# Where the loaded halves of 512-column products lie, relative to the streamed ones, modulo 128 words

## The chip, the cores and the metric

The kernel runs on one core of one Trainium2 chip. The metric is the device time of one execution in microseconds (us), smaller is better. Before the change the median of three runs is 1668.29 us (1668.05 to 1669.01).

## What is computed

Two blocks of a network over 256 tokens of width 1024, all in float32. The first block ends with a layer of 16,384 small experts, the second block has two layers that each end in a gated feed-forward part. The change touches the operands of two kinds of products in them, both of which are wide sums of products:

```python
# first block, experts: per token 8 x 16 experts are chosen, each adds coef * its row of expert_up
u = expert_down[eidx]
a = jax.nn.gelu(jnp.einsum('thkd,td->thk', u, xb), approximate=False)
coef = (g * a.astype(jnp.float32)).astype(xb.dtype)
return jnp.einsum('thk,thkd->td', coef, expert_up[eidx])

# second block, at the end of each of its two layers, D_FF = 2816
u, v = jnp.split(hn @ w_up, 2, axis=-1)
...
return (jax.nn.silu(uc) * v) @ w_down
```

## The kernel before

**Split products.** A float32 product runs as three matmuls. Each operand is held as a high part, rounded to the format `fp32r`, and the rest, its low part; the three matmuls are high by high, high by low, low by high, all added in one bank of PSUM. ScalarE (ACT) makes the high parts, VectorE (DVE) the low ones by a subtraction. A matmul of TensorE has two operands in SBUF: the **load**, 128x128 words that are put into the array (rows PEld of the profile), and the **stream**, 128x256 or 128x512 words that pass through it (rows PE). While one matmul streams, the load of the next one runs. In the rows a matmul is written `bank<-stream,load`: `bank<-hi_u,chi` streams `hi_u` and has `chi` loaded.

**First pass and second pass of the experts.** `expert_down` and `expert_up` come in 256 units of 128x1024 words; two units are a pair. In the first pass (units 0 to 127, `down_unit`, lines 940 to 944) a unit is the load and the activations `xh`, `xl` are the stream, 256 columns at a time. In the second pass (units 128 to 255, `up_half`, lines 987 to 989) the coefficients of the pair are the load, and the unit is the stream, 512 columns at a time: for each unit, two blocks of tokens by two halves of the columns by three matmuls, so 12 matmuls, 24 for a pair, 1536 for 64 pairs. The coefficients of pair 0 are `chi0` and `clo0`; those of the others are `chi[:, q % 2]` and `clo[:, q % 2]`, made by ACT in `coef_high` (line 1622) and by DVE in `coef_low` (line 2324). The function `pair_halves(q)` (line 371) hands them to all three. The units' high parts are in `hi_u` (three places), their low parts in `lo_u` and, in the second pass for odd units, in `lo_up` (`low_unit`, line 377).

**Feed-forward parts.** `ffn(layer, res)` first makes the gated activations, whose high and low parts are `gh0`, `gl0` or `gh1`, `gl1` (`gated_of`, lines 408 to 412). Then 11 slots of `w_down` are streamed, 512 columns at a time, with the gated parts loaded: 11 slots by 4 banks by 2 by 3 matmuls, 264 for a layer, 528 for both. All go through the helper `three` (lines 607 to 609).

**Places.** SBUF is laid out by hand with `Area`, counted in words of 4 bytes in each partition. `beside(at, by)` moves the next tensor forward until its place is `at + by` modulo 128. All streamed weights and units (`whi`, `wlo`, `hi_u`, `lo_u`, `lo_up`) are congruent to `HIGH_AT` = 13264, and every slice that a matmul takes of them, or of the loads below, begins a multiple of 128 words into it. What is left is one number for each product, the place of its load minus the place of its stream, modulo 128, called the **offset** here:

| product | stream, load | columns | offset |
|---|---|---|---|
| second pass, lines 987 to 989 | units, `chi` and `clo` | 512 | 0 |
| down product of both layers, lines 607 to 609 | `w_down`, `gh` and `gl` | 512 | 0 |
| first pass, lines 940 to 944 | `xh` and `xl`, units | 256 | 16 |
| `up0`, `up1`, `pq`, `xq` | `nh` and `nl`, weights | 256 | 16 |
| `out`, `xo`, `even_out`, `odd_out` | weights, `xmh` and `xml` | 256 | 16 |
| the last chunks of `in` (`w_v`, `w_o`) | weights, `xh` and `xl` | 256 | 112 |
| `xv` | weights, `memh` and `meml` | 256 | 112 |

What orders the work: TensorE runs its list in program order. In the second pass a unit's high part waits for `unit_used`, which the first matmul of a later unit sets; the coefficients of pair q wait for the unit that last read their place.

Of the kernel before, what the change touches and what calls it, by code (L numbers as in the profile page):

```python
# [29 lines left out]
F32R = mybir.dt.float32r  # L30
# [8 lines left out]
T = 256  # L39
# [158 lines left out]
def program(nc, t):  # L198
    with ExitStack() as ctx:
# [49 lines left out]
        HIGH_AT = keep.at  # L249
# [99 lines left out]
        chi0 = first_pair("chi0", 2, T, dt=F32R)  # L349
        clo0 = first_pair("clo0", 2, T, dt=F32R)  # L350
# [9 lines left out]
        spread_g = units("spread_g", TB, P, P)  # L360
        assert units.at == WORDS
        crossing = Area(CROSSING_AT)
        crossing.beside(HIGH_AT, 0)
        lo_up = crossing("lo_up", UNIT, dt=F32R)
        crossing.beside(HIGH_AT, 0)
        chi = crossing("chi", 2, 2, T, dt=F32R)
        clo = crossing("clo", 2, 2, T, dt=F32R)
        g_final = crossing("g_final", D)
        assert crossing.at <= CROSSING_AT + 2 * KD * T + 128

        def pair_halves(q):
            return (chi0[:, :, :], clo0[:, :, :]) if q == 0 else (chi[:, q % 2, :, :], clo[:, q % 2, :, :])

        def by_block(x):
            return x.rearrange("p c (b t) -> p b c t", b=TB)
# [30 lines left out]

        f5 = Area(ARENA2 + 128)
        gated_of = []
        for layer_, by in ((0, 0), (1, 0)):
            halves = Area(ARENA2)  # L410
            halves.beside(HIGH_AT, by)
            gated_of.append((halves(f"gh{layer_}", 22, T, dt=F32R), halves(f"gl{layer_}", 22, T, dt=F32R)))
# [144 lines left out]
        def _(pe):  # L557
# [424 lines left out]
            def up_half(c, w, half, tb):  # L982
                q, j = c // 2, c % 2
                tok = slice(tb * P, (tb + 1) * P)
                c_hi, c_lo = [x[:, j, tok] for x in pair_halves(q)]
                out, cs = banks[2 * half + tb][:, :], slice(half * 512, (half + 1) * 512)
                first = pe.matmul(out, c_hi, w[0][:, cs], start=(c == 0), stop=False)  # L987
                pe.matmul(out, c_hi, w[1][:, cs], start=False, stop=False)  # L988
                mm = pe.matmul(out, c_lo, w[0][:, cs], start=False, stop=(c == P - 1))  # L989
                if c == P - 1:  # L990
                    cur["b"] = of[2 * half + tb]
                    close(mm)
                return first
# [323 lines left out]
        def _(act):  # L1317
# [299 lines left out]
            def coef_high(q):  # L1617
                act.wait_ge(S("coef_made"), q + 1)
                if q >= 3:

                    act.wait_ge(S("unit_used"), P + 2 * (q - 2) + 2)
                a(A(by_block(pair_halves(q)[0]), spread_g[:, :, 2 * q:2 * q + 2, :], ACT.Copy), S("coef_high"))
# [215 lines left out]
        def _(dve):  # L1838
# [482 lines left out]
            def coef_low(q):  # L2321
                dve.wait_ge(S("coef_high"), q + 1)
                hi, lo = pair_halves(q)
                v(V.tensor_tensor(by_block(lo), spread_g[:, :, 2 * q:2 * q + 2, :], by_block(hi).bitcast(F32), ALU.subtract),
                  S("coef_low"))
# [441 lines left out]
def build(nc, arrays):  # L2767
    t = {}
    for name, a in arrays.items():
        t[name] = nc.dram_tensor(f"in_{name}", a.shape, F32, kind="ExternalInput").ap()  # L2770
    t["aside"] = nc.dram_tensor("aside", (PAIRS, P, 2 * T), F32, kind="Internal").ap()
    t["out"] = nc.dram_tensor("out", (T, D), F32, kind="ExternalOutput").ap()
    program(nc, t)
# [11 lines left out]
```

## Time and profile before

| | |
|---|---|
| median of three runs | 1668.29 us |
| the profiled execution | 1663.66 us |
| its span, first to last instruction | 1661.8 us |
| TensorE busy (PE) | 1643.4 us, 99% |
| VectorE busy (DVE) | 1237.7 us, 74% |
| ScalarE busy (ACT) | 935.5 us, 56% |

All rows are of the profiled execution. It is 4.63 us shorter than the median of the runs. A matmul's own duration in the rows is longer than its share of the time, since a matmul's pipeline overlaps the next; the time that a matmul costs is the distance from its start to the start of the next, called its **step** here. It is read from the starts in the timeline, or from a stretch as its length plus one duration, divided by the matmuls that touch it.

### The profile page before, as it was taken

The page shows a single profiled execution, that of the slowest core. Times are in us where ns is not written, and L with a number is a line of the kernel's source. Part 1 is how long each engine was busy: PE and PEld are TensorE (multiplying, and loading weights), DVE is VectorE, ACT ScalarE, POOL GpSimd, SP SyncE. Part 2 cuts the span into 40 slices and gives each one's busy share as a digit, 9 for nine tenths or more (in the row PEclk, how much of TensorE's full clock was granted, in tenths as well). Part 3 has the DMA queues.
Part 4 walks back from the last instruction along what each step waited for, and adds up shares of the span by engine and source line. Part 5 has one row for each costly group of instructions (what it writes and reads, how often), then busy time and mean ns, then how long its engine had stood idle before and what let it go on. Part 6 is the DMA issues. An engine that isn't in the chain of part 4 may idle for free.

```text
span 1661.8 us, 30280 instructions
## 1 busy us (share of the span) xinstructions
PE 1643.4 (99%) x12006; PEld 1536.2 (92%) x12006; DVE 1237.7 (74%) x1896; ACT 935.5 (56%) x1139; POOL 242.4 (15%) x333
## 2 busy tenths in 40 slices
PE   8999999999999999999999999999999999999999
PEld 8999999999999999988888888999999888899997
DVE  6875467999998666666767767887899565779974
ACT  7786565555555555554554554786655357565542
POOL 0000000004667767301101100000000000100000
PEclk9999999999999999999999999999999999999999
DMA  8444344776555555777777776633555544345553
GB/s 306 153 153 177 106 178 142 236 237 213 188 177 190 186 191 190 270 242 242 240 245 238 240 248 221 234 127 127 194 191 199 190 168 150 127 157 201 202 188 117
DMA packets 73804, 323.40 MB, mean 195 GB/s; under 512 B 8663, under 2 KB 9047, under 8 KB 55744
## 3 DMA queue, kind: packets, MB, share of 16 engines
q1 hardware_dynamic: 58736, 285.18, 50.4%
q0 software_dynamic: 5568, 19.38, 3.8%
q10 hardware_dynamic: 9360, 16.92, 2.7%
q8 instruction: 95, 1.56, 0.4%
q14 instruction: 45, 0.37, 0.1%
HBM read 303.62 MB, written 17.83 MB: 193 GB/s over the span
## 4 chain that ended last, share of the span: by engine, by line
PE 82%; DVE 12%; ACT 4%; issue 1%; DMA 0%; SPq 0%; ACTq 0%; DVEq 0%
PE bank L607 13%; PE bank L609 13%; PE bank L608 13%; PE bank L987 7%; PE bank L988 7%; PE bank L989 7%; PE bank L940 5%; PE bank L944 5%; PE bank L943 5%; DVE lo_u L2301 3%; PE bank L952 2%; DVE wlo L1916 2%; DVE oh L2312 2%; ACT whi L1352 1%; DVE pos L2198 1%
## 5 line engine op out<-in xcount | busy, mean ns | idle before, releaser
L1588 ACT ACTIVATE hi_u<-raw_u 128x1024 fp32r<-128x1024 f32 x256 | 271.9, 1062 | 276.4 <-PE bank L987 160.6
L1916 DVE TENSOR_TENSOR wlo<-raw,whi 128x2048 fp32r<-128x2048 f32 (+1 forms) x141 | 314.7, 2232 | 100.8 <-PE bank L607 77.9
L1352 ACT ACTIVATE whi<-raw 128x2048 fp32r<-128x2048 f32 x137 | 263.2, 1921 | 72.7 <-PE bank L607 69.6
L940 PE MATMUL bank<-xh,hi_u 128*128 128x256 f32 x1024 | 291.6, 285 | 1.3 <-DVE lo_u L2301 0.9
L2301 DVE TENSOR_TENSOR lo_u<-raw_u,hi_u 128x1024 fp32r<-128x1024 f32 x192 | 237.9, 1239 | 67.9 <-PE bank L940 61.6
L943 PE MATMUL bank<-xl,hi_u 128*128 128x256 f32 x1024 | 285.0, 278 | 0.0
L944 PE MATMUL bank<-xh,lo_u 128*128 128x256 f32 x1024 | 284.9, 278 | 0.0
L607 PE MATMUL bank<-nh,whi 128*128 128x256 f32 x904 | 251.7, 278 | 0.7 <-DVE wlo L1916 0.6
L608 PE MATMUL bank<-nl,whi 128*128 128x256 f32 x904 | 250.2, 277 | 0.0
L609 PE MATMUL bank<-nh,wlo 128*128 128x256 f32 x904 | 250.2, 277 | 0.0
L521 POOL TENSOR_SCALAR oh<-kept,sel_T 128x128 f32<-128x128 f32 x256 | 199.5, 795 | 249.2 <-ACT sel_T L1638 165.6
L987 PE MATMUL bank<-hi_u,chi 128*128 128x512 f32 x512 | 199.4, 389 | 0.3 <-DVE lo_up L2301 0.3
L989 PE MATMUL bank<-hi_u,clo 128*128 128x512 f32 x512 | 199.2, 389 | 0.0
L940 PEld LDWEIGHTS bank<-xh,hi_u 128*128 128x128 f32 x1024 | 192.6, 188 | 3.8 <-DVE lo_u L2301 1.7
L943 PEld LDWEIGHTS bank<-xl,hi_u 128*128 128x128 f32 x1024 | 193.5, 189 | 0.0
L944 PEld LDWEIGHTS bank<-xh,lo_u 128*128 128x128 f32 x1024 | 192.7, 188 | 0.0
L607 PEld LDWEIGHTS bank<-nh,whi 128*128 128x128 f32 x904 | 169.8, 188 | 1.7 <-DVE wlo L1916 1.5
L608 PEld LDWEIGHTS bank<-nl,whi 128*128 128x128 f32 x904 | 170.0, 188 | 0.0
L609 PEld LDWEIGHTS bank<-nh,wlo 128*128 128x128 f32 x904 | 169.9, 188 | 0.0
L2301 DVE TENSOR_TENSOR lo_up<-raw_u,hi_u 128x1024 fp32r<-128x1024 f32 x64 | 78.4, 1226 | 94.5 <-PE bank L987 92.9
L607 PE MATMUL bank<-whi,nh 128*128 128x256 f32 x408 | 115.5, 283 | 0.8 <-DVE nl L1897 0.7
L987 PEld LDWEIGHTS bank<-hi_u,chi 128*128 128x128 f32 x512 | 96.1, 188 | 20.6 <-DVE lo_up L2301 0.7
(417 smaller groups left out, 3353.8 us busy)
## 6 DMA issues: line engine op xcount, KB each, us to landing
raw<-in_weights SPq DMA_DIRECT2D x138, 1024.0 KB, 4.8
raw_u<-in_experts SPq DMA_DIRECT2D x256, 512.0 KB, 4.2
aside<-a_out ACTq DMA_DIRECT2D x64, 256.0 KB, 3.7
a_in<-aside POOLq DMA_DIRECT2D x64, 256.0 KB, 3.7
const<-in_const SPq DMA_DIRECT2D x1, 1409.0 KB, 9.0
const<-in_const POOLq DMA_DIRECT2D x1, 1409.0 KB, 7.2
h<-in_x SPq DMA_DIRECT2D x2, 512.0 KB, 5.2
raw<-in_weights SPq DMA_DIRECT2D x2, 512.0 KB, 7.9
```

The source lines that it names most:

```text
L607: freeing(pe.matmul(out, lhs[0], rhs[0], start=first, stop=False, skip_group_check=skip))
L608: pe.matmul(out, lhs[0], rhs[1], start=False, stop=False, skip_group_check=skip)
L609: return pe.matmul(out, lhs[1], rhs[0], start=False, stop=last, skip_group_check=skip)
L940: mm = pe.matmul(out, w[0][:, kp], xh[:, k, :], start=(k == 0), stop=False)
L943: pe.matmul(out, w[0][:, kp], xl[:, k, :], start=False, stop=False)
L944: mm = pe.matmul(out, w[1][:, kp], xh[:, k, :], start=False, stop=(k == KD - 1))
L987: first = pe.matmul(out, c_hi, w[0][:, cs], start=(c == 0), stop=False)
L989: mm = pe.matmul(out, c_lo, w[0][:, cs], start=False, stop=(c == P - 1))
L1352: a(A(whi[:, n % HIGH, :], raw[:, n % RAW, :], ACT.Copy), S("weights_hi"))
L1588: a(A(hi_u[:, u % HIGH_U, :], raw_u[:, u % RAW_U, :], ACT.Copy), S("unit_high"))
L1916: v(V.tensor_tensor(wlo[:, n % LOW, place], raw[:, n % RAW, place], whi[:, n % HIGH, place].bitcast(F32), ALU.subtract), S("weights_split" ...
L2301: v(V.tensor_tensor(low_unit(u), raw_u[:, u % RAW_U, :], hi_u[:, u % HIGH_U, :].bitcast(F32), ALU.subtract), S("unit_split"))
```

## The change

The coefficients of the second pass are no longer two tensors with two places each but `odd_pair` and `even_pair`, each with its high and its low part. `odd_pair` lies at offset 96 and `even_pair` at offset 112; pair 0 keeps `chi0` and `clo0` at offset 0. `lo_up` now lies behind them, at offset 0 to `HIGH_AT` as before. The gated parts lie at offset 64 in layer 0 and at 80 in layer 1. No instruction is added, taken out or reordered, and no wait is changed; only addresses are.

```diff
         crossing = Area(CROSSING_AT)
+        crossing.beside(HIGH_AT, 96)
+        odd_pair = crossing("odd_pair", 2, 2, T, dt=F32R)
+        crossing.beside(HIGH_AT, 112)
+        even_pair = crossing("even_pair", 2, 2, T, dt=F32R)
         crossing.beside(HIGH_AT, 0)
         lo_up = crossing("lo_up", UNIT, dt=F32R)
-        crossing.beside(HIGH_AT, 0)
-        chi = crossing("chi", 2, 2, T, dt=F32R)
-        clo = crossing("clo", 2, 2, T, dt=F32R)
         g_final = crossing("g_final", D)
         assert crossing.at <= CROSSING_AT + 2 * KD * T + 128
 
         def pair_halves(q):
-            return (chi0[:, :, :], clo0[:, :, :]) if q == 0 else (chi[:, q % 2, :, :], clo[:, q % 2, :, :])
+            halves = odd_pair if q % 2 else even_pair
+            return (chi0[:, :, :], clo0[:, :, :]) if q == 0 else (halves[:, 0, :, :], halves[:, 1, :, :])
...
-        for layer_, by in ((0, 0), (1, 0)):
+        for layer_, by in ((0, 64), (1, 80)):
             halves = Area(ARENA2)
             halves.beside(HIGH_AT, by)
```

## Rows read from the trace of the kernel before

**Rows 1.** The page, parts 1 and 2: busy time, TensorE's clock.
```profile
PE 1643.4 (99%) x12006; PEld 1536.2 (92%) x12006; DVE 1237.7 (74%) x1896; ACT 935.5 (56%) x1139; POOL 242.4 (15%) x333
PEclk9999999999999999999999999999999999999999
```

**Rows 2.** The page, part 4: the chain that ended last.
```profile
PE 82%; DVE 12%; ACT 4%; issue 1%; DMA 0%; SPq 0%; ACTq 0%; DVEq 0%
```

**Rows 3.** The page, part 5: costliest groups, two of the second pass.
```profile
L987 PE MATMUL bank<-hi_u,chi 128*128 128x512 f32 x512 | 199.4, 389 | 0.3 <-DVE lo_up L2301 0.3
L989 PE MATMUL bank<-hi_u,clo 128*128 128x512 f32 x512 | 199.2, 389 | 0.0
```

**Rows 4.** Who waited for whom, 691 to 1034 us: in total, times, longest.
```profile
ACT hi_u L1588 <- PE bank L987: 160.6, 122, 1.7
DVE lo_up L2301 <- PE bank L987: 91.4, 62, 1.5
ACT hi_u L1588 <- DMA raw_u<-in_experts: 2.9, 2, 2.7
DVE clo L2324 <- ACT chi L1622: 1.2, 2, 0.7
```

**Rows 5.** Timeline of TensorE in the second pass: start, length, instruction.
```profile
799.82 0.39 PE L987 MATMUL bank<-hi_u,chi 128*128 128x512 f32 x1
...
801.18 0.39 PE L987 MATMUL bank<-hi_u,chi 128*128 128x512 f32 x1
```

**Rows 6.** Stretches of the span, TensorE alone: length, busy time, matmuls; clock; DMA.
```profile
700.00:1030.00 330.00, 330.00 (x1458) 1.00 0.75 243
1309.00:1348.00 39.00, 39.00 (x174) 1.00 0.59 210
1200.00:1280.00 80.00, 80.00 (x708) 1.00 0.55 194
150.00:168.00 18.00, 18.00 (x155) 1.00 0.53 183
59.00:70.00 11.00, 11.00 (x96) 1.00 0.29 97
73.00:78.00 5.00, 5.00 (x46) 1.00 0.63 228
111.00:116.00 5.00, 5.00 (x45) 1.00 0.80 238
177.00:187.00 10.00, 10.00 (x87) 1.00 0.29 107
```

**Rows 7.** Groups by line and form, TensorE alone: the down products of both layers.
```profile
L607 PE MATMUL bank<-whi,gh 128*128 128x512 f32 x176 | 68.8, 391 | 0.0
```

**Rows 8.** One line's instructions, L896: a product of unsplit float32, 256 columns.
```profile
L896 PE MATMUL bank<-xT,vx x32: 379/379/382, 190.1 to 196.8; 128*128 128x256 f32 x32
```

**Rows 9.** Timeline of TensorE, from `up0` into the down product of layer 0.
```profile
1290.43 0.28 PE L607 MATMUL bank<-nh,whi 128*128 128x256 f32 x1
...
1290.77 0.39 PE L607 MATMUL bank<-whi,gh 128*128 128x512 f32 x1
1291.00 0.40 PE L608 MATMUL bank<-wlo,gh 128*128 128x512 f32 x1
1291.23 0.39 PE L609 MATMUL bank<-whi,gl 128*128 128x512 f32 x1
1291.47 0.39 PE L607 MATMUL bank<-whi,gh 128*128 128x512 f32 x1
1291.69 0.39 PE L608 MATMUL bank<-wlo,gh 128*128 128x512 f32 x1
```

**Rows 10.** Timeline of TensorE, the end of a chunk of `out` and the transposes behind it.
```profile
134.03 0.28 PE L609 MATMUL bank<-whi,xml 128*128 128x256 f32 x1
134.15 0.60 PE L594 MATMUL bank<-kept,h 128*128 128x128 f32 x4
```

## The prediction

> **What bounds the kernel now.** I read the busy times first, then the chain of waits, then the stretches of TensorE. TensorE is busy 99% of the span at the full granted clock, which is its level of 2.4 GHz [rows 1], and the chain that ended last is 82% TensorE [rows 2]. So the kernel is a list of matmuls, and what counts is the step from one start to the next. In the second pass no one keeps TensorE waiting: its groups have 0.3 us and 0.0 us of idle time before them [rows 3], while ACT waits 160.6 us and DVE 91.4 us for it between 691 and 1034 us [rows 4]. A change in the steps of that pass therefore moves the end one for one, in both directions, and the same holds for the down products.
>
> The step of a 512-column matmul is steady. From 799.82 to 801.18 us six steps take 1.36 us, 226.7 ns each [rows 5]. Over the whole pass, 700 to 1030 us, it is (330 + 0.389) / 1458 = 226.6 ns; in the down product of layer 0 it is (39 + 0.389) / 174 = 226.4 ns [rows 3, 6]. Both are at offset 0. The 256-column matmuls have **two levels**. In `up0` (offset 16, 1200 to 1280 us) the step is (80 + 0.28) / 708 = 113.4 ns; in `pq` (the same offset, 150 to 168 us) it is (18 + 0.28) / 155 = 117.9 ns. At offset 112 the stretches from 59, 111 and 177 us give 117.5, 117.3 and 118.2 ns, and only the one from 73 us is lower, 5.28 / 46 = 114.8 ns, an upper bound with its edges [rows 6]. I call these the fast and the slow level; between them lie 117.7 - 113.4 = 4.3 ns. The reader should see two things: that the slow level exists at both offsets but is much the more common one at 112 (26 us of 31 in the four stretches), and that 226.6 ns is just two times 113.3 ns.
>
> **The change part by part.** It changes no instruction and no wait, only addresses. The count of steps that it can touch: pairs 1, 3, ... 63 are 32 pairs by 24 = 768 matmuls at offset 96; pairs 2 to 62 are 31 by 24 = 744 at offset 112; 264 each at 64 and 80 in the two down products (176 by 3 = 528 for both [rows 7]). In all 2040. Pair 0, with 24, stays.
>
> *Writing the halves.* ACT and DVE write the same shapes to new addresses. I cost that at nothing: they are covered by the 160.6 and 91.4 us in which these engines wait for TensorE [rows 4]. Without that cover a slower write of a pair's coefficients would count 64 times; DVE waited for ACT's high parts just 1.2 us in all, twice [rows 4].
>
> *`lo_up` moves behind the pairs*, from the place of `xh` to that of `xl`. Both are last read by the first pass's last unit, and the same wait guards it; its offset is unchanged. Nothing.
>
> *The step of 2040 matmuls.* No row shows a 512-column product of this kind at another offset for more than a moment, so it is bounded from both sides.
> From below: if the 226.6 ns hold a stall that another offset removes, what is left is a stream without it. The nearest row is the unsplit float32 product of 256 columns: 31 steps in 196.8 - 190.1 = 6.7 us, 216.1 ns [rows 8]. It passes half as many columns, each slower, so it is a far row, but it is the only full-clock stream of that length with a shorter step. That bounds the gain at 226.6 - 216.1 = 10.5 ns a matmul, 2040 by 10.5 = 21.4 us.
> From above: the load of 128x128 words can slow only the part of the stream beside which it runs. Where a 512-column stretch begins there are rows of just that: the first steps of the down product take 1291.00 - 1290.77 = 0.23, 0.23 and 0.24 us, 0.70 us for three, 233 ns each, and the fourth is back at 0.22 us [rows 9]. That is 6 to 7 ns above the level, and near 113.3 + 117.7 = 231.0 ns, one half of the stream at the slow level and one at the fast. So I price the slow level at 4.3 ns a matmul, one half affected, and at most at 2 by 4.3 = 8.6 ns, both halves: 8.8 us and 17.5 us over 2040.
> The value that I take is **nothing**. The reason is the second thing above: 113.3 ns for 256 columns at offset 16 and 226.6 ns for 512 at offset 0 are the same time per column, although a load runs beside nearly all of the one stream and beside only a part of the other, and at different offsets. A stall between load and stream would not scale with columns. So 226.6 ns reads as a plain rate of the stream, from which no offset can take anything. And in a 512-column stretch the three slow steps cure themselves in under 1 us [rows 9], where a 256-column stretch stays slow for 18 us [rows 6]. The load has about half of the step to spare here; I take it that this slack lets it fall into the fast level at other offsets too.
>
> On this the Trainium skill speaks twice. "TensorE: Matmul & The Clock Gate" (Step-by-step: what each phase is for) says that TensorE has two independent SBUF read ports, so that loading the next weights takes no read bandwidth from the running matmul. By that rule no offset matters and the sum is nothing; the two levels of [rows 6] at one and the same shape speak against its being the whole story. The same page (Back-to-back issue gap) gives N/2.4 + 2.5 ns, an estimate of 215.8 ns for 512 columns; the trace has 226.6. If all of the difference could be had, the sum would be some 22 us.
>
> **Sum.** 0 + 0 + 0: the profiled execution stays at 1663.66 us and the median at 1668.3 us. What may move without a change of step: later 256-column stretches start at another moment and may fall into the other level. The up stages and `even`, `odd` after 1040 us hold about 600 us; if one stretch as long as that of `pq`, 18 us, changes level, that is 155 by 4.3 = 0.7 us; three of them one way are 2 us.
>
> **The rivals.**
> *The slow level takes hold* (slower). Beside the load, the stream runs at the slow level at offsets other than 0. Its place is the first part of each of the 2040 steps, its price 4.3 ns. For it: 26 of 31 us at offset 112 are slow [rows 6], and 744 matmuls go to that offset; and where the last matmul of a chunk has as the next load the transpose's `h`, at offset 48, its step is 134.15 - 134.03 = 0.12 us [rows 10], the slow side of the two levels. Against it: the self-cure above. At all four offsets: 2040 by 4.3 = 8.8 us, 1677.1 us. At 112 alone: 744 by 4.3 = 3.2 us, 1671.5 us. At 112 and 96: 1512 by 4.3 = 6.5 us, 1674.8 us. It decides the sign from 3.3 / 0.0043 = 770 matmuls on. With both halves at all offsets: 1668.3 + 17.5 = 1685.8 us.
> *A stall is removed* (faster). 226.6 ns is not a rate but holds a meeting of load and stream at offset 0, absent at some of 64 to 112. Full price 21.4 us, 1646.9 us; on one of the two kinds of pair, 8 us, 1660.3 us. For it: the float32 row. Against it: the equal time per column.
> *Offsets differ both ways* and cancel: the four values are four different cases, and one number comes out. This falls between the others.
>
> **How the numbers follow.** A measurement of this kernel tells about 0.2%, 3.3 us, from no change. No effect of the offset, or effects on too few matmuls: 0.46, at 1668.3 us, its own range 1666 to 1671. Slow level on 770 matmuls or more: 0.42, most of it 1672 to 1677, a small part to 1686. A removed stall: 0.12, 1647 to 1665. I forecast the first, 1668.3 us. The range leaves out about one in ten on either side: 1664 cuts off the larger gains, 1679 lies above the slow level at all four offsets and below both halves of it.
>
> **What would show it.** Steps of 226.6 ns from 700 to 1030 us (x1458 in that stretch) and in both down products say that I am right. Steps that alternate by pair, every 24 matmuls, say that the offset counts: 231 ns is the slow rival, anything below 226 ns the fast one; the two down products give offsets 64 and 80 by themselves. If the second pass grows and ACT and DVE wait less for TensorE, it is a writer and not the matmul. The prediction is wrong if the load's slack does not let it into the fast level, or if equal time per column was chance.

## The result, and the profile after

The change makes the kernel slower. The median of 16 runs is 1676.32 us (1671.33 to 1679.09), beside 1668.1 us for 16 runs of the kernel before (1661.77 to 1669.43). The ratio is 1.0053, 95% interval 1.0042 to 1.0063, so 8.8 us, between 7.0 and 10.5 us. The profiled execution took 1671.59 us, its span is 1669.8 us, 8.0 us longer than before. Executions of one and the same kernel spread over some 8 us, so where an experiment below has one execution of each kernel (1 to 4, 8 and 9), its time is only a rough sign, and the argument rests on the steps in its trace.

The page's parts 1 and 2, after (the lines that answer to [rows 1]):

```profile
PE 1653.0 (99%) x12006; PEld 1538.0 (92%) x12006; DVE 1237.5 (74%) x1896; ACT 935.5 (56%) x1139; POOL 242.0 (14%) x333
PEclk9999999999999999999999999999999999999999
```

TensorE's busy time grew by 9.6 us with the same 12006 matmuls at the same clock; DVE's and ACT's did not move. Who waited for whom between 691 and 1041 us, after (beside [rows 4]):

```profile
ACT hi_u L1590 <- PE bank L989: 168.7, 123, 1.7
DVE lo_up L2303 <- PE bank L989: 96.2, 63, 1.6
DVE odd_pair L2326 <- ACT odd_pair L1624: 1.2, 2, 0.7
```

ACT and DVE wait longer for TensorE than before (160.6 and 91.4 us, in a pass some 7 us shorter), and DVE waits for ACT's halves 1.2 us as before, so it is not the writers of the halves. The stretches of TensorE, after, in the columns of [rows 6]; the second pass, the down product of layer 0, that of layer 1, and `up0`:

```profile
700.00:1030.00 330.00, 330.00 (x1430) 1.00 0.75 240
1316.00:1354.00 38.00, 38.00 (x169) 1.00 0.59 213
1624.00:1662.00 38.00, 38.00 (x165) 1.00 0.35 126
1200.00:1280.00 80.00, 80.00 (x708) 1.00 0.56 197
```

In the second pass 1430 matmuls stand where there were 1458: 330.39 / 1430 = 231.0 ns a step. Layer 0, at offset 64, has 38.39 / 169 = 227.2 ns; layer 1, at 80, 38.39 / 165 = 232.7 ns. `up0` is as before, 708 matmuls. The timeline of the second pass, after (start, length, instruction), tells the pairs apart:

```profile
810.09 0.39 PE L990 MATMUL bank<-lo_u,odd_pair 128*128 128x512 f32 x1
...
812.89 0.39 PE L990 MATMUL bank<-lo_up,odd_pair 128*128 128x512 f32 x1
...
813.80 0.39 PE L991 MATMUL bank<-hi_u,even_pair 128*128 128x512 f32 x1
...
817.92 0.39 PE L991 MATMUL bank<-hi_u,even_pair 128*128 128x512 f32 x1
```

Twelve steps of an odd pair take 2.80 us, 233.3 ns each; eighteen of an even pair 4.12 us, 228.9 ns each; before, both took 226.7 ns [rows 5]. Taken over all starts of the profile, the means are:

| steps | before | after | count | cost |
|---|---|---|---|---|
| odd pairs, offset 96 | 226.7 ns | 233.0 ns | 768 | 4.8 us |
| even pairs, offset 112 | 226.7 ns | 229.1 ns | 744 | 1.8 us |
| down product of layer 0, offset 64 | 226.9 ns | 226.9 ns | 264 | 0 |
| down product of layer 1, offset 80 | 226.8 ns | 233.3 ns | 264 | 1.7 us |

The sum is 8.3 us, beside the 8.0 us by which the span of the profiled execution grew, and inside the interval of the runs.

These are means. Single steps alternate in a pattern: by their starts to the nanosecond, an odd pair at 96 takes 229 and 237 in turn, an even pair at 112 takes 226, 229 and 232, layer 1 at 80 takes 230 or 231 and 236, where offset 0 has only 226 and 227. The last step of an odd pair takes 232 in place of 237 ns, and that is why 96 shows 233.0 and not 233.3 over all starts.

### The profile page after: what moved, and what is told of

It reads as the page before. It is cut to its first block, busy times and chain, and to the rows that moved or that the text cites. A ratio compares the mean times of both kernels' runs of the same rounds, so it can differ in the third digit from the quotient of the medians.

```text
span 1669.8 us, 30280 instructions
## 1 busy us (share of the span) xinstructions
PE 1653.0 (99%) x12006; PEld 1538.0 (92%) x12006; DVE 1237.5 (74%) x1896; ACT 935.5 (56%) x1139; POOL 242.0 (14%) x333
## 4 chain that ended last, share of the span: by engine, by line
PE 82%; DVE 12%; ACT 4%; issue 1%; DMA 0%; SPq 0%; ACTq 0%; DVEq 0%
PE bank L609 13%; PE bank L610 13%; PE bank L611 13%; PE bank L991 7%; PE bank L990 7%; PE bank L989 7%; PE bank L942 5%; PE bank L945 5%; PE bank L946 5%; DVE lo_u L2303 3%; PE bank L954 2%; DVE wlo L1918 2%; DVE oh L2314 2%; ACT whi L1354 1%; DVE pos L2200 1%
## 5 line engine op out<-in xcount | busy, mean ns | idle before, releaser
L610 PE MATMUL bank<-wlo,nh 128*128 128x256 f32 x408 | 113.2, 277 | 0.0
L611 PE MATMUL bank<-whi,nl 128*128 128x256 f32 x408 | 113.1, 277 | 0.0
L989 PE MATMUL bank<-hi_u,odd_pair 128*128 128x512 f32 x256 | 101.3, 396 | 0.2 <-DVE lo_up L2303 0.2
```

The costliest lines, as they stand in the source:

```text
L610: pe.matmul(out, lhs[0], rhs[1], start=False, stop=False, skip_group_check=skip)
L611: return pe.matmul(out, lhs[1], rhs[0], start=False, stop=last, skip_group_check=skip)
```

## The experiments

The theory after the result: a 512-column step depends on the offset of the load from the stream and on nothing else of their places. The stream's own place is the same modulo 128 in all 512-column products of all runs here; only the load was moved. So for 512 columns no run tells the offset from the place of the load alone. For 256 columns the rows do: with the loads at the place of `HIGH_AT` and the stream 16 words below it (`up0`), and with the stream there and the loads 16 words above (`out`), the same 113.3 ns is reached for long, and with both at that place (experiment 7) the step is 120.0 ns. What else was open: is it the offset or the tensor's place; over which distance does it repeat; which of the two, the load or its own matmul, pays; and is offset 0 good for 256 columns too.

**1. Two values exchanged, and 32 and 48.**

```diff
-        crossing.beside(HIGH_AT, 96)
-        odd_pair = crossing("odd_pair", 2, 2, T, dt=F32R)
-        crossing.beside(HIGH_AT, 112)
+        crossing.beside(HIGH_AT, 48)
         even_pair = crossing("even_pair", 2, 2, T, dt=F32R)
...      # lo_up, as in the change
+        crossing.beside(HIGH_AT, 32)
+        odd_pair = crossing("odd_pair", 2, 2, T, dt=F32R)
...
-        for layer_, by in ((0, 64), (1, 80)):
+        for layer_, by in ((0, 80), (1, 64)):
```

> Second pass: odd pairs at offset 32, even pairs at 48; down product of layer 0 at 80, of layer 1 at 64 (the two values of the change, exchanged). Theory A, the step depends on the offset modulo 64: 32 gives what 96 gave (233.0 ns), 48 what 112 gave (229.1 ns), layer 0 rises to 233.3 ns and layer 1 falls to 226.8 ns. Theory B, it depends on the distance of load and stream either way round modulo 128: 32 gives 233.0 ns like 96, 48 gives 233.3 ns like 80; the layers as in A. Theory C, the places or the layers differ and not the offsets: layer 0 stays at 226.9 ns and layer 1 at 233.3 ns. By A the second pass lasts 356 us, by B 358 us; the whole by A is 8 us above the kernel before.

Measured: 1671.31 us, 7.5 us above the kernel before on the same chip. Stretches of TensorE: the second pass, layer 0, layer 1.

```profile
700.00:1030.00 330.00, 330.00 (x1430) 1.00 0.75 240
1317.00:1355.00 38.00, 38.00 (x165) 1.00 0.57 204
1624.00:1662.00 38.00, 38.00 (x169) 1.00 0.37 135
```

The counts of the two layers are those of the changed kernel, exchanged: 165 matmuls now stand in layer 0 and 169 in layer 1. So it is the place of the load and not the layer or the tensor; theory C falls. Over all starts, odd pairs at 32 have 233.0 ns, as at 96, and even pairs at 48 have 229.1 ns, as at 112. That is theory A, a period of 64 words; by theory B 48 should have given the 233.3 ns of 80.

**2. The other half of the map.** Odd pairs at 64, even pairs at 16, `((0, 32), (1, 48))` for the layers, in the lines of the diff above.

> Second pass: odd pairs at offset 64, even pairs at 16; down product of layer 0 at 32, of layer 1 at 48. Theory A (offset modulo 64): 64 gives 226.7 ns, 16 gives 233.3 ns like 80, layer 0 233.0 ns, layer 1 229.1 ns. Theory B (distance either way, modulo 128): 64 gives 226.7, 16 gives 229.1 like 112, layer 0 233.0, layer 1 233.3 ns. Theory D, that 16 is harmless since 256-column products run at 113.4 ns there: 16 gives 226.7 ns. By A the even pairs cost 744 x 6.6 = 4.9 us, by B 1.8 us, by D nothing.

Measured: 1670.00 us, 6.2 us above the kernel before (one execution each). The timeline of the second pass:

```profile
813.33 0.39 PE L989 MATMUL bank<-hi_u,even_pair 128*128 128x512 f32 x1
...
818.00 0.39 PE L991 MATMUL bank<-hi_u,even_pair 128*128 128x512 f32 x1
818.23 0.39 PE L989 MATMUL bank<-hi_u,odd_pair 128*128 128x512 f32 x1
...
820.29 0.39 PE L989 MATMUL bank<-hi_u,odd_pair 128*128 128x512 f32 x1
...
823.01 0.39 PE L989 MATMUL bank<-hi_u,odd_pair 128*128 128x512 f32 x1
```

Offset 16 costs as much as 80: twenty steps in 4.67 us, 233.5 ns. Theories B and D fall. The odd pairs at 64 do reach the low step, 2.72 us for twelve, 226.7 ns, but only after the first nine steps of the pair, which take 2.06 us, 229 ns each: after the change of offset the pair has lost about 20 ns before it settles. Over all starts 64 has 227.9 ns here, 16 has 233.3 and layer 1 at 48 has 229.1. Layer 0 at 32 has 232.4 ns, 0.6 less than the odd pairs at 32 and 96; its steps run in a longer pattern of seven (228 to 241 ns), and why is not known.

**3. One part of a pair moved.** The edit against the changed kernel; the layers are at `((0, 112), (1, 96))`.

```diff
         crossing.beside(HIGH_AT, 96)
-        odd_pair = crossing("odd_pair", 2, 2, T, dt=F32R)
-        crossing.beside(HIGH_AT, 112)
-        even_pair = crossing("even_pair", 2, 2, T, dt=F32R)
         ...
+        odd_high = crossing("odd_high", 2, T, dt=F32R)
+        even_low = crossing("even_low", 2, T, dt=F32R)
+        crossing.beside(HIGH_AT, 0)
+        odd_low = crossing("odd_low", 2, T, dt=F32R)
+        even_high = crossing("even_high", 2, T, dt=F32R)
```

> Only one part of a pair's coefficients is moved. Odd pairs: high part at offset 96, low part at 0. Even pairs: high part at 0, low part at 96. Down products: layer 0 at 112, layer 1 at 96. If the cost arises where the load of the next matmul runs beside a stream, it lies on the steps whose next load is moved: in odd pairs on L989 and L991 (next load high), not on L990 (next load low), so about (233 + 227 + 233) / 3 = 231 ns on average; in even pairs on L990 alone, (227 + 233 + 227) / 3 = 229 ns. If it arises with a matmul's own load, the odd pairs are slow on L989 and L990 and the even ones on L991. If it is a matter of one pair's parts lying together, it is gone. Layer 0 at 229.1 ns and layer 1 at 233.0 ns, if the pass and the down products obey one rule.

Measured: 1675.17 us, 11.4 us above the kernel before (one execution each). Stretch of the second pass, and an even pair in the timeline (the three lines of a product are L990 to L992 in this kernel):

```profile
700.00:1030.00 330.00, 330.00 (x1421) 1.00 0.74 239
```

```profile
816.22 0.39 PE L990 MATMUL bank<-hi_u,even_high 128*128 128x512 f32 x1
...
820.38 0.39 PE L990 MATMUL bank<-hi_u,even_high 128*128 128x512 f32 x1
```

The second pass has 330.39 / 1421 = 232.5 ns a step, 231.0 in the changed kernel. The two are not alike, since the even pairs of the changed kernel are at 112; with both parts of every pair at 96 it would be 233.0. The 18 steps shown of an even pair take 4.16 us, 231.1 ns each. Over all starts the three lines have 226.7, 232.5 and 235.0 ns in the even pairs (231.4 in the mean) and 233.6, 232.7 and 234.5 in the odd ones (233.6). So an odd pair with one part moved is no shorter than one with both.

Taken apart: in an even pair the step beside which the moved low part is loaded (L991 here) is slow, and the first is not, as expected of a meeting of stream and next load; but L992, beside which an unmoved part is loaded, is slower still. In an odd pair all three are slow. So neither expectation holds. Whether a step pays for the load before it, as its own matmul or as an after-effect like the one at the start of a pair in experiment 2, is left open. The layers at 112 and 96 have 229.2 and 232.4 ns, as the layers at 48 and 32 in experiment 2.

**4. Between the multiples of 16.** Odd pairs at 8, even pairs at 72, layers at 40 and 120.

> Offsets between the multiples of 16. Second pass: odd pairs at 8, even pairs at 72; down product of layer 0 at 40, of layer 1 at 120. If only blocks of 16 words count, 8 behaves like 0 or 16 (226.7 or 233.3 ns) and 72 like 64 or 80 (the same two), 40 like 32 or 48, 120 like 112 or 0. If the step varies smoothly with the offset, 8 and 72 lie near 230 ns, 40 near 231 and 120 near 228 ns. By Theory A 8 and 72 are equal.

Measured: 1676.52 us, 12.8 us above the kernel before (one execution each). Second pass, layer 0, layer 1:

```profile
700.00:1030.00 330.00, 330.00 (x1416) 1.00 0.75 238
1321.00:1359.00 38.00, 38.00 (x165) 1.00 0.58 208
1629.00:1667.00 38.00, 38.00 (x164) 1.00 0.35 126
```

330.39 / 1416 = 233.3 ns, the same for 8 and for 72, which is the period of 64 again; 40 and 120 have 233.3 ns too. So the map is no smooth curve and no matter of blocks of 16: of the places tried, 0 has 226.7 ns, 48 has 229.1, 32 has 232.4 to 233.0, and all others have 233.3.

**5. All wide products at 64.** Both pairs and both layers at 64.

> The change with 64 in place of 96, 112 and 80: both pairs and both down products at offset 64, 256-column products as before. Theory A: steps of 226.7 ns in the whole second pass and both down products, time as the kernel before within 0.1%. If pairs laid out the new way, or lo_up's new place, cost anything by themselves, it is the excess here: up to 8 us.

```profile
700.00:1030.00 330.00, 330.00 (x1458) 1.00 0.75 244
```

Measured: 1664.21 us (median of 12), ratio to the kernel before 1.0002 (0.9992 to 1.0012). The stretch holds the 1458 matmuls of [rows 6]. The new layout of the pairs and `lo_up`'s new place cost nothing that the interval shows (2.0 us at most), and 64 is as good as 0.

**6. The pairs alone.** 96 and 112 for the pairs, both layers back at 0.

> One part of the change alone: pairs at 96 and 112, both down products back at offset 0. From the profile of the changed kernel: 768 x 6.3 ns + 744 x 2.4 ns = 6.6 us longer than the kernel before, and 264 x 6.5 ns = 1.7 us shorter than the change. Second pass of 356 us. If later 256-column stretches matter more than the steps themselves, the difference to before lies outside 5 to 8 us.

Measured: 1670.01 us (median of 6), ratio 1.0033 (1.0020 to 1.0046), so 5.5 us (3.3 to 7.7) where the steps give 6.6. The second pass has 1429 matmuls in the stretch of 330 us, and the layers are at 226.9 and 226.8 ns. The part of the layers is 1.7 us by its steps. What is left of the whole 8.8 us is 3.3 us; the intervals of the two ratios, about 2 us either way each, hold the 1.7 but do not show it.

**7. 256 columns at 0, and at 64.** The kernel before, with `xh`, `xmh`, `memh`, `nh1` and `nh4` to `nh7` and their low parts at one place:

```diff
-        for n_, by in ((4, 16), (5, -16), (6, 16), (7, -16)):
+        for n_, by in ((4, 0), (5, 0), (6, 0), (7, 0)):
-        m1.beside(HIGH_AT, -16)
+        m1.beside(HIGH_AT, 0)
-        p3.beside(HIGH_AT, -16)
+        p3.beside(HIGH_AT, 0)
-        keep.at += 64
+        keep.at += 80
         XH = keep.at
...
-        keep.at += 64
-        mixed = Area(XH + 32)
+        keep.at += 48
+        mixed = Area(XH)
```

The second kernel has them all at 64 by the same lines. What was expected, for 0 and for 64:

> The kernel before, with the 256-column products too at offset 0 (before they were at 16, and at 112 in a few chunks); 512-column ones stay at 0. In the profile of before some 2960 of 8430 steps of 256 columns stand at the slow level, 4.3 ns above the fast one, 12.7 us in all. Theory A carried over (0 modulo 64 is where the load costs the stream nothing, whatever the width): nearly all steps at 113.3 ns, the kernel 8 to 13 us shorter than before, about 1656 us. Rival E (at 256 columns the load fills the step, and the level is set by how a stretch begins, not by the offset): share of slow steps and time as before, 1668 us. Rival F (16 was the better place for 256 columns): more slow steps, up to 23 us longer if all are slow.

> As the kernel with all 256-column products at offset 0, but at 64; 512-column ones stay at 0. By a period of 64 words its time is that of the kernel with 0, within 2 us, and its shares of slow steps are alike. If the period holds only at 512 columns, the two differ.

Measured: 1695.99 us and 1696.13 us (five executions each), ratio 1.0189 for both (1.0174 to 1.0204). I had hoped to gain 8 to 13 us and lost 31.6. Stretches of the kernel with 0, `up0` and `pq`:

```profile
1205.00:1285.00 80.00, 80.00 (x669) 1.00 0.54 193
150.00:168.00 18.00, 18.00 (x152) 1.00 0.50 179
```

80.28 / 669 = 120.0 ns. Of some 8500 steps, 7845 with 0 and 7852 with 64 are 120 ns to the nanosecond: a third level, above both of [rows 6]. Over the starts the 256-column steps are 44.5 us longer in the trace of the kernel with 0 than before, and its span 31.9 us: the other 12.6 us are made up for in the other products and in steps that hold a wait. The period of 64 words holds at 256 columns too, but the map is another: the place that is best for 512 columns is the worst seen here. Theory A carried over and rival E fall. Rival F was right, and its "up to 23 us" too low, as I had priced it with the level of 117.7 ns.

**8. The map of 256 columns.** `by` 24, -8, 40 and 8 for `nh4` to `nh7`, and `xh` at -32, in the lines of the diff above.

> The kernel before with its 256-column products at other offsets, one in each stage; 512-column ones stay at 0. First pass and the first chunks of in at 32, even at 24, up0 at 8, odd at 40, up1 at 56; pq, the memory products and the residual products stay at 16. Known so far at 256 columns: 0 and 64 give 120.0 ns always, 16 gives 113.3 or 117.7 ns by stretch, 112 (48 modulo 64) mostly 117.7 ns. Theory G (a stream loses when it meets the load, and the further the load lies from 0 modulo 64, the less): 32 is the best, 113.3 ns throughout the first pass, which is then some 6 us shorter; 24 and 40 nearly so; 8 and 56 lie between 117 and 120 ns. Theory H (only blocks of 16 words count): 24 behaves like 16 or 32, 8 and 56 like 0 or 16. Theory I (16 alone is good): every other value gives 117 ns or more, and the kernel is 10 to 20 us longer than before.

Measured: 1683.61 us, 15.4 us above the kernel before (one execution each). Stretches: `up0` at 8, `up1` at 56.

```profile
1205.00:1285.00 80.00, 80.00 (x678) 1.00 0.53 185
1500.00:1580.00 80.00, 80.00 (x687) 1.00 0.57 198
```

They give 118.4 and 116.9 ns. Over all starts: the first pass at 32 has 119.5 ns, `even` at 24 has 117.8, `odd` at 40 has 119.9. Theories G and H fall: 32 is near the worst, and 8 and 56 have levels of their own. Theory I holds but for its "117 ns or more", which 56 passes by a hair (116.7 ns), and for offset 112 (48 modulo 64), where the kernel before has one stretch of 46 steps at 113.3 ns (73 to 78 us) that has not come back in any later kernel. Only 16 reaches that level for long. No version that beats the kernel before came out of this.

**9. The second pass cut to 256 columns.** The same tensors, each stream in two parts of 256 columns with a load each; odd pairs at 0 and even ones at 16, then at 32 and 48, the layers at 0.

```diff
-                first = pe.matmul(out, c_hi, w[0][:, cs], start=(c == 0), stop=False)
-                pe.matmul(out, c_hi, w[1][:, cs], start=False, stop=False)
-                mm = pe.matmul(out, c_lo, w[0][:, cs], start=False, stop=(c == P - 1))
+                for part in range(2):
+                    o = out[:, part * T:(part + 1) * T]
+                    cs = slice(half * 512 + part * T, half * 512 + (part + 1) * T)
+                    ...   # the same three matmuls, into o
```

> Width changed, everything else kept: in the second pass each 512-column stream is cut into two of 256 columns, each with its own load, over the same tensors (3072 matmuls in place of 1536). Odd pairs at offset 0, even pairs at 16; down products as before. Theory W (the width decides which offset costs): the odd pairs take 120.0 ns a step, 2 x 120.0 = 240.0 ns in place of 226.7; the even pairs 113.3 to 117.7 ns, 2 x 113.3 = 226.7 ns in place of the 233.3 that 512 columns take there, so the order of 0 and 16 turns round. The pass lasts 350 + 768 x 13.3 ns = 360 us with even pairs at the fast level, 367 us at the slow one. Rival P (it lies in these tensors or this pass): offset 0 is still the shorter one.

> The same cut of the second pass into 256-column streams, odd pairs at offset 32, even pairs at 48. By the map of 256 columns (first pass at 32: 119.5 ns; memory products at 48: 117.8 ns) the odd pairs take 119.5 ns and the even ones 117.8 ns a step. Rival: the map of 256 columns was a matter of its stages, then the steps are others.

Measured: 1687.93 us with 0 and 16, 1678.42 us with 32 and 48, beside 1669.06 us for the kernel before (one execution each). The timeline of the first:

```profile
802.06 0.28 PE L993 MATMUL bank<-hi_u,odd_pair 128*128 128x256 f32 x1
...
807.70 0.28 PE L996 MATMUL bank<-hi_u,odd_pair 128*128 128x256 f32 x1
807.82 0.28 PE L993 MATMUL bank<-hi_u,even_pair 128*128 128x256 f32 x1
```

The pair at 0 takes 5.76 us for 48 steps, 120.0 ns each; over all starts the pairs at 16 have 117.8 ns, those at 32 and 48 have 118.7 and 117.8. So in the very tensors where 0 beats 16 at 512 columns (226.7 against 233.3 ns), 16 beats 0 at 256 (2 by 117.8 against 2 by 120.0 ns). It is the width, with the load that each part has, that turns the order round. The even pairs stayed at the slow of the two levels of offset 16 throughout.

The map, mean step in ns over all starts of a stage, all from the kernels above:

| offset modulo 64 | 0 | 8 | 16 | 24 | 32 | 40 | 48 | 56 |
|---|---|---|---|---|---|---|---|---|
| 512 columns | 226.7 | 233.3 | 233.3 | | 232.4 to 233.0 | 233.3 | 229.1 | 233.3 |
| 256 columns | 120.0 | 118.3 | 113.3 or 117.7 | 117.8 | 118.7 to 119.5 | 119.9 | 117.8, once 113.3 | 116.7 |

## Why the prediction was right or wrong

**What bounds the kernel.** Right. TensorE's list of matmuls is the kernel, and 8.3 us of longer steps made the span 8.0 us longer.

**Which costs were nothing.** Right for the writers of the halves and for `lo_up`: experiment 5 has all of that and the time of before.

**The step.** Here the forecast failed. I took nothing as the value, and the step that failed is the last of that part, "I take it that this slack lets it fall into the fast level at other offsets too". The changed kernel and experiments 1 to 4 show in its place a step that is fixed by where the load lies: 233.3 ns at 80, 233.0 at 96 and 229.1 at 112, and no stretch at these ever settled at 226.7 ns. The slack itself was not read from a row. The rows of the loads, before, in the second pass and in `up0`:

```profile
L987 PEld LDWEIGHTS bank<-hi_u,chi 128*128 128x128 f32 x485 | 91.0, 188 | 18.9
L607 PEld LDWEIGHTS bank<-nh,whi 128*128 128x128 f32 x236 | 44.3, 188 | 0.0
```

A load is recorded with 188 ns beside steps of 226.7 and of 113.3 ns alike. Beside the short step it cannot all be time that the load keeps to itself, so these rows do not say how much of a step is spare, half or less. The self-cure that I read off [rows 9] is real: by their starts to the nanosecond those three steps take 232, 232 and 231, then 227. But it took place at offset 0, and in experiment 2 too a pair settles at the step of its own offset; it tells nothing of another one.

The reason ahead of it, that 113.3 and 226.6 ns are the same time per column at different offsets, was half right. No offset that was tried gave 512 columns less than 226.7 ns, so the faster rival found no support. But I compared 256 columns at 16 with 512 at 0, which are the lowest values found in each map. At one and the same offset the time per column is not equal: at 0 it is 120.0 against 226.7 ns, at 16 it is 113.3 or 117.7 against 233.3. The equality is one of the two lowest values, and I read it as if the offset did not matter.

**The rivals.** The slower one took place. Its number for all four offsets, 1677.1 us, is 0.8 us from the median, but its terms were wrong and met in the sum: it had 4.3 ns for each of 2040 matmuls, and the four offsets cost 0 (at 64), 2.4 (at 112), 6.3 (at 96) and 6.5 ns (at 80). That the number came out is luck. It leaned on the rows of 256 columns at 112; by those rows 112 is worse than 16, and 0 was never seen, while at 512 columns 112 is the mildest of the three that cost, and 0 at 256 columns is the worst. A map of one width says nothing of the other. "At 112 alone" would have been 744 by 2.4 = 1.8 us. The fourth rival, that the four values differ, was right that they are different cases, and wrong that they could cancel: one is zero, three are losses.

**The range**, 1664 to 1679 us, held the median of 1676.3 us only since it reached to that rival; the inner range of the value that I forecast, 1666 to 1671 us, did not.

**What would show it.** Steps that alternate by pair, each 24 matmuls, and two layers with two values: this is what the trace has, and it priced four offsets in one profile.

On the rule that I weighed: the Trainium skill, "TensorE: Matmul & The Clock Gate" (Step-by-step: what each phase is for), has loads and streams on independent read ports, with no bandwidth taken from the running matmul. The runs here differ: addresses alone move a 512-column step between 226.7 and 233.3 ns and a 256-column one between 113.3 and 120.0 ns. The formula of the same page's section "Back-to-back issue gap", an estimate of 215.8 ns for 512 columns, was reached at no offset; the lowest mean is 226.7 ns.

## What to carry to other kernels

Where TensorE is the bound and each matmul has its own load, as in these `fp32r` products (no other format was tried), the distance of the load's address from the stream's, modulo 64 words, is worth up to 3% of a 512-column step (233.3 against 226.7 ns) and up to 6% of a 256-column one (120.0 against 113.3 ns). It has to be measured for each width: in this kernel 0 is the place for 512 columns and 16 for 256. One profile maps several offsets at once, if different stages or alternating buffers get different ones; and a level read off one width or one offset should not be carried to another without a run.

## What was not expected of the hardware

The means of a settled stretch fall on a grid of about 6.67 ns, an estimate from the rows: 113.3, 120.0, 226.7 and 233.3 ns are 17, 18, 34 and 35 of these; at the slow level of 256 columns three steps hold 53 (117.7 ns each), and in a pair at 112 three steps hold 103 (226, 229 and 232 ns, time and again). Single steps do not: at 96 they take 229 and 237 ns in turn, and at 56, with 256 columns, the mean of 116.7 ns is 17.5 of them. What this grid is, and why 256 columns at offset 16 have two lasting levels, no run here settles. Places nearer than 8 words to each other were not tried, as the tensors of this kernel begin at multiples of 8 words. Nor was it told apart whether the cost in experiment 3 lies with the load beside a stream or with the one before it, or, at 512 columns, whether the stream's own place counts, as it was never moved. What in the chip makes the offset count stays open; what is shown is that addresses alone move the step.
